# A decoder layer's first branch: other orders at its seams, and the token sums on GpSimd

## The reference

```
branch_a = (attn * silu(a_z)) @ w_branch_attn
branch_m = (sigmoid(m_o) * h_m * silu(m_z)) @ w_branch_mlstm
merged   = sigmoid(g_attn) * branch_a + sigmoid(g_mlstm) * branch_m
out      = rms_norm(x + merged @ w_out, final_norm_w)
```

## Time and profile before

| | |
|---|---|
| median of three runs | 1094.22 us |
| profiled execution | 1094.62 us |
| its span | 1092.9 us |
| mean granted clock of TensorE | 0.992 |
| TensorE busy | 97% |
| VectorE, GpSimd, ScalarE busy | 71%, 63%, 49% |

### The profile page before, as it was taken

One profiled execution on the slowest core, in us unless ns is written; L12 is line 12 of the kernel. 1 busy time (PEld: TensorE's weight loads), 2 busy tenths in 40 slices (PEclk: granted clock), 3 DMA queues, 4 the chain that ended last, 5 costly groups with the idle time before them and its releaser, 6 DMA issues.

```text
span 1092.9 us, 18700 instructions
## 1 busy us (share of the span) xinstructions
PE 1060.9 (97%) x6343; PEld 858.0 (79%) x6343; DVE 777.1 (71%) x1188; ACT 538.4 (49%) x1283; POOL 683.4 (63%) x465
## 2 busy tenths in 40 slices
PE   8999999999999999999999999999998999899997
PEld 6887887877877888888888888888776787677786
DVE  5965785866867866768676767677768557647797
ACT  7544755646646634553455435554565434103443
POOL 3577556555565578568866886678459963446341
PEclk9999999999999999999999999999999999989999
DMA  6233142152231233333332432242266359645424
GB/s 217 82 85 82 40 126 68 42 159 51 77 106 40 97 97 90 101 93 103 87 89 81 131 86 77 71 149 78 78 209 215 106 202 346 212 148 216 175 86 145
DMA packets 120972, 129.67 MB, mean 119 GB/s; under 512 B 7804, under 2 KB 97208, under 8 KB 119368
## 3 DMA queue, kind: packets, MB, share of 16 engines
q1 hardware_dynamic: 107384, 89.66, 26.9%
q10 hardware_dynamic: 13520, 39.13, 10.6%
HBM read 95.12 MB, written 33.65 MB: 118 GB/s over the span
## 4 chain that ended last, share of the span: by engine, by line
PE 81%; DVE 5%; DMA 5%; POOL 4%; ACT 2%; issue 1%; DVEq 1%; POOLq 1%; ACTq 0%; SPq 0%
PE ps L1077 62%; PE ps L984 4%; PE ps L1195 3%; POOL ring_lo L834 2%; PE ps L1381 2%; PE ps L1176 2%; PE ps L1250 2%; DMA w_raw<-in_w_branch_mlstm 2%; DMA f_again<-s_scratch 1%; PE ps L1322 1%; PE ps L1304 1%; DMA u_raw<-u_sums_scratch 1%; DVE u_m L2643 1%; ACT ev L1471 1%; PE ps L1319 1%
## 5 line engine op out<-in xcount | busy, mean ns | idle before, releaser
L834 POOL TENSOR_TENSOR ring_lo<-w,ring_hi 128x512 fp32r<-128x512 f32 x144 | 212.9, 1499 | 93.1 <-ACT ring_hi L1513 93.1
L834 POOL TENSOR_TENSOR ring_lo<-t,ring_hi 128x512 fp32r<-128x512 f32 x108 | 152.9, 1420 | 146.7 <-ACT ring_hi L1513 146.7
L1077 PE MATMUL ps<-s_hi,ring_hi 128*128 128x512 f32 x576 | 228.6, 397 | 0.0
L1077 PE MATMUL ps<-s_lo,ring_hi 128*128 128x512 f32 x576 | 225.1, 391 | 0.0
L1077 PE MATMUL ps<-s_hi,ring_lo 128*128 128x512 f32 x576 | 225.0, 391 | 0.0
L1077 PE MATMUL ps<-h_hi,ring_hi 128*128 128x512 f32 x432 | 171.6, 397 | 8.2 <-POOL ring_lo L834 5.2
L1077 PE MATMUL ps<-h_lo,ring_hi 128*128 128x512 f32 x432 | 169.7, 393 | 0.0
L1077 PE MATMUL ps<-h_hi,ring_lo 128*128 128x512 f32 x432 | 169.2, 392 | 0.0
L1513 ACT ACTIVATE ring_hi<-w 128x512 fp32r<-128x512 f32 x144 | 86.6, 622 | 112.4 <-PE ps L1077 102.2
L1077 PEld LDWEIGHTS ps<-s_hi,ring_hi 128*128 128x128 f32 x576 | 108.2, 188 | 23.5 <-issue 2.5
L1077 PEld LDWEIGHTS ps<-s_hi,ring_lo 128*128 128x128 f32 x576 | 108.2, 188 | 22.5
(11 more groups left out here) (311 smaller groups left out, 2076.0 us busy)
## 6 DMA issues: line engine op xcount, KB each, us to landing
w<-in_w_in SPq DMA_DIRECT2D x128, 256.0 KB, 3.0
xs<-in_x SPq DMA_DIRECT2D x8, 512.0 KB, 7.5
ga_scratch<-ev ACTq DMA_DIRECT2D x4, 1024.0 KB, 4.2
u_scratch<-silu_z ACTq DMA_DIRECT2D x8, 512.0 KB, 3.2
c_rows<-c_scratch ACTq DMA_DIRECT2D x8, 512.0 KB, 6.8
ev<-u_scratch SPq DMA_DIRECT2D x8, 512.0 KB, 4.7
u_sums_scratch<-ev ACTq DMA_DIRECT2D x4, 1024.0 KB, 4.2
gm_scratch<-ev ACTq DMA_DIRECT2D x4, 1024.0 KB, 5.2
```

What stands on the lines that cost most here:

```text
L834: return nc.gpsimd.tensor_tensor(flat(lo[:]), flat(raw_or_sum[:]), flat(hi[:]).bitcast(F32), ALU.subtract)
L1077: mm = nc.tensor.matmul(ps[:, bank, columns], w[:, k, :], h[:, k, columns], start=(m == 0), stop=(m == PRODUCT - 1))
```

## The change

**Sums of the tokens.** `branch_sums` leaves VectorE and is run by GpSimd, as a `hook` in `sums(i + 1)` of the third pair of each set, between `w12`'s sum and the low part of `w11`. ScalarE stores them one chunk later (chunk 4), in the last set at chunk 7. GpSimd's loop over the pairs is partly written out.

**Seam into the first branch.** SP loads `w11` and `w21` of pair 32 ahead of block 0 and does not wait for `p1_done` before them. ScalarE makes the blocks' high parts in other places: 0 and 1 after the fourth pair's second product, 2, 3, 4 after its products 5, 6, 7, and 5, 6 in pair 32, so block 2 comes after `high_1` of pair 32; the store of the last `g_mlstm` rows comes after the third product. VectorE's low parts follow. In pair 32 GpSimd makes the low part of `t4` ahead of that of `w22`.

**Gates of the last pair.** The `ga` rows of the last pair are asked for after the high parts of `u_m`.

**Stores.** The six stores of the output weights' blocks go from SP's list (between the loads of the second branch's weights) to ScalarE's (n = 3 and n = 5 of its loop).

**Reloads.** SP brings `o22` back ahead of the wait for the seventh merged tile.

```diff
-            def branch_weights(a, src=wba_cols):
+            def branch_weights(a, between=None):
                 n1, n2 = ROWS_OF[a]
-                pair_weights(WPAIRS + a, n1 * P, n2 * P, src=src)
+                pair_weights(WPAIRS + a, n1 * P, n2 * P, src=wba_cols, between=between)
...
-            sp.wait_ge(p1_done, WPAIRS)
-            tokens_block(0)
-            branch_weights(0)
+            def first_block():
+                sp.wait_ge(p1_done, WPAIRS)
+                tokens_block(0)
+
+            branch_weights(0, first_block)
...
                 weights(BM + 2 * i, [(0, wbm_cols, 2 * P * i)])
                 if i == 1:
                     output_weights([(1, f_o22), (1, f_o12)])
-                if i == 3:
-                    sp.wait_ge(wo_sum, 4)
-                    sp.dma_start(scr_s[1], f_s4[:]).then_inc(wo_stored, 16)
-                    sp.wait_ge(wo_sum, 5)
-                    for part, src in enumerate((part_hi, s3_lo)):
-                        sp.dma_start(scr_split[1, part], src[:].bitcast(F32)).then_inc(wo_stored, 16)
                 weights(BM + 2 * i, [(1, wbm_cols, P + 2 * P * i)])
-                if i == 1:
-                    sp.wait_ge(wo_sum, 1)
-                    sp.dma_start(scr_s[0], f_s1[:]).then_inc(wo_stored, 16)
-                    sp.wait_ge(wo_sum, 3)
-                    for part, src in enumerate((part_hi, o22_lo)):
-                        sp.dma_start(scr_split[0, part], src[:].bitcast(F32)).then_inc(wo_stored, 16)
...
-            sp.wait_ge(merged_ready, KT - 1)
-            sp.dma_start(ev[:, 0, :], x_rows[:, 0, :]).then_inc(x_in[0], 16)
-
             sp.wait_ge(wo_stored, 16 * 6)
             sp.wait_ge(um_free, 1)
             for part in range(2):
                 sp.dma_start(o22[part][:].bitcast(F32), scr_split[0, part]).then_inc(wo_again[0], 16)
+            sp.wait_ge(merged_ready, KT - 1)
+            sp.dma_start(ev[:, 0, :], x_rows[:, 0, :]).then_inc(x_in[0], 16)
             sp.wait_ge(um_free, 3)
...
-            def sums(i):
+            def sums(i, hook=None):
...
                 add(w12[:], w22[:], w12[:], ALU.subtract).then_inc(sum_made, 1)
+                if hook is not None:
+                    hook()
...
+            def branch_sums(p):
+
+                pool.wait_ge(us_in, 32 * (p + 1))
+                a11, a21, a12, a22 = [ev[:, j, token_half(h)] for j in range(2) for h in range(2)]
+                nc.gpsimd.tensor_tensor(a22, a21, a22, ALU.add)
+                nc.gpsimd.tensor_tensor(a21, a11, a21, ALU.subtract)
+                pool.drain()
+                nc.gpsimd.tensor_tensor(a11, a22, a11, ALU.subtract)
+                pool.drain()
+                nc.gpsimd.tensor_tensor(a12, a12, a11, ALU.subtract).then_inc(us_made, 1)
+
+            weights_of_pair(0)
+            with pool.Fori(1, 15) as i:
+                weights_of_pair(i)
+            for i in range(15, WPAIRS):
+                p, place = divmod(i - 13, 5)
+                weights_of_pair(i, hook=(lambda p=p: branch_sums(p)) if place == 2 else None)
+            weights_of_pair(WPAIRS, new_tokens=True)
+            for i in range(WPAIRS + 1, SPAIRS):
+                weights_of_pair(i)
...
-                us_chunk = 4 if last else 3
+                us_chunk = 7 if last else 4
...
-                    if last and q:
-                        block_high(q - 1)
+                    if last and q == 1:
+                        block_high(0)
+                        block_high(1)
+                    if last and q >= 4:
+                        block_high(q - 2)
...
-                    if q == 0 and a == 0:
-                        block_high(6)
+                    if a == 0 and q in (0, 1):
+                        block_high(5 + q)
+                    if a == 0 and q == 2:
                         store_gm(PAIRS - 1)
-                    if q == 3:
+                    if q == 3 and not last:
...
                             A(um_part(k)[0], um_full(k), ACT.Copy).then_inc(u_hi, 1)
+                        act.wait_ge(a_gated, 2 * a)
+                        for j in range(2):
+                            gate_row(j, scr_a, ROWS_OF[a][j])
...
+                if n == 3:
+                    act.wait_ge(wo_sum, 1)
+                    act.dma_start(scr_s[0], f_s1[:]).then_inc(wo_stored, 16)
+                    act.wait_ge(wo_sum, 3)
+                    act.drain()
+                    for part, src in enumerate((part_hi, o22_lo)):
+                        act.dma_start(scr_split[0, part], src[:].bitcast(F32)).then_inc(wo_stored, 16)
...
+                if n == 5:
+                    act.wait_ge(wo_sum, 4)
+                    act.dma_start(scr_s[1], f_s4[:]).then_inc(wo_stored, 16)
+                    act.wait_ge(wo_sum, 5)
+                    act.drain()
+                    for part, src in enumerate((part_hi, s3_lo)):
+                        act.dma_start(scr_split[1, part], src[:].bitcast(F32)).then_inc(wo_stored, 16)
...
-                    if last and 2 <= q <= 4:
+                    if last and q in (2, 3):
                         block_low(q - 2)
+                    if last and q == 5:
+                        block_low(2)
                     if last and q == 6:
                         block_low(3)
+                        block_low(4)
```

More of the change, by code:

```diff
@@ L606, in _, with pair_weights @@
             sp.dma_start(before_rc[:, :], scr_before.rearrange("h (c a) -> (h c) a", a=1)).then_inc(g_moved, 16)
-            def pair_weights(i, n1, n2, first=False, src=w_cols):
+            def pair_weights(i, n1, n2, first=False, src=w_cols, between=None):
                 n = i if isinstance(i, int) else sp.snap(i)
@@ L619, in pair_weights @@
                 sp.dma_start(w21[:], src[:, KH:KT, ds(c1, P)]).then_inc(w21_in, 16)
+                if between is not None:
+                    between()
                 sp.wait_ge(w7_ready, n)
@@ L871, in _, with weights_of_pair @@
             sums(0)
-            def weights_of_pair(i):
+            def weights_of_pair(i, new_tokens=False, hook=None):
                 pool.wait_ge(w2_hi, i + 1)
@@ L877, in weights_of_pair @@
                 low(w12, ring3).then_inc(w7_ready, 1)
-                pool.wait_ge(w3_hi, i + 1)
-                low(w22, ring4).then_inc(w3_ready, 1)
+                if not new_tokens:
+                    pool.wait_ge(w3_hi, i + 1)
+                    low(w22, ring4).then_inc(w3_ready, 1)
                 pool.wait_ge(w4_hi, i + 1)
                 low(t4, ring0).then_inc(w4_ready, 1)
+                if new_tokens:
+                    pool.wait_ge(w3_hi, i + 1)
+                    low(w22, ring4).then_inc(w3_ready, 1)
                 pool.wait_ge(w5_hi, i + 1)
@@ L884, in weights_of_pair @@
                 if not final(i, SPAIRS):
-                    sums(i + 1)
-            ended(pool, SPAIRS, weights_of_pair)
+                    sums(i + 1, hook)
+            def branch_sums(p):
[16 more added lines that the diff above has]
+                weights_of_pair(i)
             for j in range(2):
@@ L2520, in silu_z_part @@
                         .then_inc(mz_used, 1)
-                us_chunk = 3 if last else 2
-                def branch_sums():
-                    dve.wait_ge(us_in, 32 * (p + 1))
-                    dve.sem_inc(passed, 1)
-                    a11, a21, a12, a22 = [ev[:, j, token_half(h)] for j in range(2) for h in range(2)]
-                    V.tensor_tensor(a22, a21, a22, ALU.add)
-                    V.tensor_tensor(a21, a11, a21, ALU.subtract)
-                    dve.drain()
-                    V.tensor_tensor(a11, a22, a11, ALU.subtract)
-                    dve.drain()
-                    V.tensor_tensor(a12, a12, a11, ALU.subtract).then_inc(us_made, 1)
                 def advance(c):
@@ L2580, in mlstm_step @@
                         denominators(c - 1)
-                    if c == us_chunk:
-                        branch_sums()
                     if c < NB:
@@ L2649, in _ @@
                     if a == 0:
-                        if q == 0:
-                            block_low(4)
                         if q == 1:
```

## The result

The changed kernel takes 1075.72 us in the median of four runs (1074.52 to 1077.1), beside 1093.84 us for the kernel before (1090.61 to 1096.98, four runs): ratio 0.9835, 95% interval 0.9802 to 0.9867, 18.1 us less. The profiled execution took 1074.72 us with a span of 1073.0, 19.9 us under the earlier trace rows. Forecast were 1074.3 us and a span 19.9 shorter. The total was right; its terms were not all so. Part 2 gave about half of its term, part 1 and the stretch from the fifth tile to the output gave more, and parts 4 and 5, summed as two causes, turned out to be two cures for one wait.

The account below looks back on a forecast made before the run. TensorE's own stream plus gaps and slow-clock stretches was taken as the bound, 26.9 us recoverable at most. 2.7 - 0.3 + 2.6 + 1.3 + 10.3 + 3.3 = 19.9 us off 1094.6, less 0.4, gave 1074.3 us; own range 1070 to 1079, wider 1067 to 1085.

Parts of the forecast that it names:

- Part 2: Seam into the first branch: reordered weights, blocks and low parts start GpSimd 2.5 us earlier; 2.6 us, ends 0.5 and 9.0.
- Part 1: Token sums from VectorE to GpSimd: two TensorE waits in the last set go, 2.7 us, less 0.3 for sets one to three.
- Part 4: Output weight stores from SP to ScalarE's queue: late `w_raw` loads of the fifth and eighth tile leave in time; 10.3 us.
- Part 5: Reloads before the output: 2 MB leave 2.9 us earlier, clearing TensorE's wait and slow stretch; 3.3 us, ends 0 and 3.6.
- the -0.3 for them: Sets one to three: 0.1 us lost per set to GpSimd's adds.
- the cover: Third set: low part of `w11` ends 2.7 us before TensorE wants it; gone from 2.0 us per add on.
- Rival (c): GpSimd late in each of the first three sets at 3.34 us per add, low part ending about 686.3; 1100 us, chance 0.04.
- PE gets what GpSimd's start gets: First seam: GpSimd's chain is the bound, so TensorE gains what its earlier start gains; taken as 2.6 us.
- near 1.5: Sign at the first seam: gap before the first branch pair near 1.5 us, GpSimd still without a break behind it.
- Part 3: Last pair's `ga` rows asked for after the conversions: TensorE's wait for `u_m` goes; 1.3 us, bounds 0 and 1.3.
- its lead: Second branch: gates applied about 1 us later, yet `tile_out` for the third tile still about 1 us ahead of TensorE.
- the gap above 0.3 us that the forecast excluded: Sign for the stores: no TensorE gap above 0.3 us from 925 us to the end of the eighth tile.

Follow-up runs that it names:

- u_sums: The changed kernel with the branch sums of all four sets back on VectorE at the old chunks; 1079.18 us, ratio 0.9842.
- x_adds4: The changed kernel with four more GpSimd adds of a zero column, each with a drain, amid the branch sums of each set; 1083.65 us.
- u_seam: The changed kernel with all edits at the seam into the first branch undone (weights, blocks, low parts, gm store); 1075.86 us, ratio 0.9819.
- u_gates: The changed kernel with the last pair's `ga` rows asked for amid the `u_m` loads again; 1075.82 us, ratio 0.9818.
- b_stores: The kernel before with only the six stores of the output weights moved to ScalarE's queue; 1080.12 us, ratio 0.986.
- u_reload: The changed kernel with the first two reloads of the output weights behind the wait for the seventh merged tile again; 1074.69 us, ratio 0.9806.
- u_stores: The changed kernel with the six stores of the output weights back on SP; 1092.47 us, ratio 0.9958.
- b_reload: The kernel before with only the two reloads of `o22` moved ahead of the wait for `merged_ready`; 1093.95 us, ratio 0.9992.

## Why the prediction was right in its sum and not in all its terms

- **Part 1: right, a little small.** Forecast 2.4 net, 2.9 by the chunk step, 3.5 to 4.9 by u_sums, since a later TensorE also fares worse in the seam. TensorE has no gap in the first three sets, so the -0.3 for them was not needed, and the cover was 3.4 us and not 2.7 (x_adds4). Rival (c)'s end at 686.3 takes 2.6 us for the low part without saying so; with 1.29 it would be 685.0. The sums in the third set, the last two of four (the first two take 1.30 each), at the 1.4 us assumed:

```profile
672.02 1.56 POOL L891 TENSOR_TENSOR ev<-ev 128x512 f32<-128x512 f32 x1
673.72 1.28 POOL L893 TENSOR_TENSOR ev<-ev 128x512 f32<-128x512 f32 x1
```

- **Part 2: the mis-sized term.** Forecast 2.6 us, measured 1.2 (rows) and 1.5 (u_seam's span; 0.1 between the medians). The step that failed is "PE gets what GpSimd's start gets". The low part of `w11` did start 2.7 us earlier on top of part 1 (814.33 for 819.92), as forecast; but the chain from it to the end of `t1` takes 21.3 us instead of 19.7, because VectorE's blocks now lie beside more of it. Moving blocks behind the weights moved the collision: the gap ahead of the first pair is 0.30 us where "near 1.5" was expected, and 2.83 stand ahead of its third product in order instead. The earlier trace rows had the sign of it in 2.3 to 2.6 us per operation; the forecast took these as the price of the operation.
- **Part 3: a little too large.** Forecast 1.3; 1.0 between the two traces, 0.3 by u_gates' trace, whose wait for `u_m` is only 0.8 us. The wait went. The third tile kept its lead as claimed (VectorE frees it at 922.8, TensorE comes at 924.3), but ahead of the fourth, which the forecast did not look at, the later gates gave 0.54 us back. This is also the gap above 0.3 us that the forecast excluded.
- **Part 4: right in mechanism and larger than its sum.** 8.9 us at the fifth tile for 8.7, the eighth tile's gap as forecast; and the output's wait with it, 15.3 us in all (b_stores). That SP's place in line was bought and not bandwidth is shown by SP's waits, 18.8, 12.9 and 11.3 us for VectorE before and none after. The Trainium skill's sentence that another issuing engine gives no bandwidth ("DMA: Bandwidth & Descriptors", section "Issuing engines are not separate DMA queues") is not at odds with it: the loads were late in leaving, not slow.
- **Part 5: right in mechanism, wrong as a term beside part 4.** Forecast 3.3; 0 in the changed kernel (u_reload), some 4 us with the stores on SP (u_stores' trace against that of the kernel before), under 2.6 by b_reload's median, with the longer gap at the eighth tile in its trace. Part 4 alone cures the wait for `o_s_lo`, and so does part 5; the sum counted both. The mistake was to stop at the last queue (the load at 1000.82) and not ask what had held `merged_ready`.
- **The sum.** Forecast 2.4 + 2.6 + 1.3 + 10.3 + 3.3 = 19.9; by the rows 2.9 + 1.2 + 1.0 + 8.9 + 5.9 = 19.9. The last two, 14.8 us, belong to part 4, which gives 15.3 by itself (b_stores); 13.6 were forecast for parts 4 and 5 together. The total came out because the output's wait was counted once, though under part 5's name, and because 1.7 us too much in parts 2 and 3 stand against 1.7 too little in the others. That these cancel is luck.

## What to carry over

Follow a late wait back until the releaser is itself on time; here the stores on a shared queue made three waits at three places, and a fix for the last of them was worth nothing once the stores had moved. Two cures for one wait are one term of a sum. Stores left on SP also took back 3 of the 5 us that the edits ahead of them had gained (u_stores): a place where a late transfer would swallow earlier gains is priced first. Where two engines take turns at a resource, count the resource's time and not either engine's chain.

## What was not expected of the hardware

- Gaps of the same length at the same place leave the clock at either level. After 2.83 us in the changed kernel it stayed at 2.4 GHz (1.00); after 2.87 us in u_gates and 2.85 in u_stores and u_reload it fell toward 1.2 GHz, as after 2.48 us in u_sums, and after 1.90 at the output of the kernel before:

```profile
824.64:830.00 5.36, 5.04 (x21) 3.90 (x22) 5.27 (x4) 2.34 (x2) 5.36 (x2) 1.00 0.54 188
```

```profile
825.70:831.00 5.30, 5.29 (x16) 4.22 (x17) 5.21 (x4) 2.24 (x2) 5.30 (x2) 0.68 0.57 203
```

  (first the changed kernel, then u_gates). The gap ahead of it does not tell them apart either: 0.30 us in the changed kernel, 1.15 in u_gates, 0.28 in u_stores. What does was not found.
- A fall of the clock costs nothing where TensorE would wait for another engine anyway. From the end of that gap to the second branch pair it is 18.44 us in the changed kernel (824.64 to 843.08), in u_reload (824.71 to 843.15), u_gates and u_stores alike, though in the last three the clock over some 5 us behind the gap was 0.68 or 0.69. There the waits for GpSimd that follow are shorter: about 1.0 us ahead of product 5 for 1.46, and neither of the two of 0.3.
- GpSimd and VectorE exclude each other instruction by instruction where both read two arrays of SBUF: 1.30, 2.28 and 3.35 us for one GpSimd operation beside VectorE instructions of none, 1024 and 2048 elements. A memset of VectorE's (1.76 us for 128x2048) costs GpSimd nothing. The Trainium skill ("SBUF — State Buffer", section "SBUF: two separate sides") has the two lock one port pair in turn, each for its whole instruction; the traces agree by these numbers.
